# Tile ends moved two rows later and spread over five rows, and 32 weight blocks read from a compact copy, in a two-block transformer kernel on one core

## The reference

```python
for l in range(DEPTH_2):                        # one layer
    x = x + hybrid_mixer(rmsnorm_2(x, norm_mix_w[l]), w_in[l], ...)       # gated delta rule | LRU, then @ w_out
    x = x + memory_cross_attention(rmsnorm_2(x, norm_xattn_w[l]), ...)    # wq, wkv, wo
    x = x + peer_ffn(rmsnorm_2(x, norm_ffn_w[l]), peer_wq[l], peer_subkeys[l], peer_u[l], peer_v[l])
return rmsnorm_2(x, norm_final_w)

def peer_ffn(h, wq, subkeys, u_tab, v_tab):     # 16384 experts of one neuron each
    q = (t @ wq).reshape(ntok, PEER_HEADS, 2, PEER_DH)
    ...                                         # two top-16 lists per head -> 8*16 = 128 expert numbers per token
    act = jax.nn.gelu(jnp.einsum('phkd,pd->phk', u_tab[ib], tb)) * gb
    return jnp.einsum('phk,phkd->pd', act, v_tab[ib])
```

## Time and profile before

| | us |
|---|---|
| median of 3 runs (4435.22 to 4448.99) | 4435.89 |
| profiled execution | 4437.59 |
| its span | 4435.8 |
| PE busy | 3636.4 (82%) |
| DVE busy | 2022.3 (46%) |
| POOL busy | 1391.2 (31%) |
| ACT busy | 1006.3 (23%) |
| first u gather to the end of the span | 2739.9 to 4435.8 |

### The profile page before, as it was taken

How to read it: one execution, slowest core, us unless ns; L and a number is a source line. 1 busy time by engine, 2 the same in 40 slices (tenths; PEclk the granted TensorE clock), 3 DMA queues, 4 the chain that set the end, 5 groups by cost and what they waited for, 6 DMA issues and landing times.

```text
span 4435.8 us, 45304 instructions
## 1 busy us (share of the span) xinstructions
PE 3636.4 (82%) x16837; PEld 2072.6 (47%) x16837; DVE 2022.3 (46%) x4634; ACT 1006.3 (23%) x2265; POOL 1391.2 (31%) x1494
## 2 busy tenths in 40 slices
PE   7788998999999778999997989767777766555655
PEld 4455534555555565444456877434544433111111
DVE  3565062623222583111125324577756555665553
ACT  3664032200000211100015122344123112112111
POOL 0000001162422000000000002656656776777776
PEclk9899999999999899999998989888889888666677
DMA  4331102222122133422212134989779998999998
GB/s 178 114 114 44 57 24 50 76 109 105 68 83 111 62 118 124 140 79 80 80 64 76 58 133 152 339 317 327 273 295 389 359 400 322 360 357 335 357 368 313
DMA packets 287765, 821.56 MB, mean 185 GB/s; under 512 B 24040, under 2 KB 60340, under 8 KB 284244
## 3 DMA queue, kind: packets, MB, share of 16 engines
q0 software_dynamic: 150832, 565.17, 34.4%
q1 hardware_dynamic: 136320, 253.22, 16.0%
q10 hardware_dynamic: 420, 0.62, 0.1%
HBM read 791.67 MB, written 27.26 MB: 185 GB/s over the span
## 4 chain that ended last, share of the span: by engine, by line
PE 57%; DVE 13%; POOL 9%; issue 8%; ACT 5%; DMA 4%; another core or an unknown queue 3%; SPq 0%; DVEq 0%; ACTq 0%; POOLq 0%
PE bank L728 25%; PE bank L2627 6%; POOL arena L1176 5%; POOL ring L1167 4%; PE bank L2863 4%; PE bank L2430 3%; PE bank L2587 3%; DVE ring L2286 2%; PE bank L2482 2%; DMA arena<-in_peer_v,arena 1%; PE bank L2345 1%; PE bank L593 1%; PE bank L2422 1%; PE bank L2722 1%
## 5 line engine op out<-in xcount | busy, mean ns | idle before, releaser
L2863 PE MATMUL bank<-arena 64*64 64x512 f32 x4096 | 684.4, 766 | 383.4 <-issue 318.5
L1167 POOL DMA_INDIRECT ring<-in_peer_u,arena x512 | 560.2, 1094 | 1389.3 <-DVE arena L2233 1061.8
L2286 DVE SCALAR_TENSOR_TENSOR ring<-ring,xT 128x1024 f32<-128x1024 f32 x512 | 615.4, 1223 | 271.7 <-DMA ring<-in_peer_u,arena 247.3
L1176 POOL DMA_INDIRECT arena<-in_peer_v,arena x512 | 581.4, 1135 | 207.3 <-issue 145.9
L2863 PEld LDWEIGHTS bank<-arena 64*64 64x64 f32 x4096 | 183.1, 160 | 800.6 <-issue 798.0
L728 PE MATMUL bank<-hT,ring 128*128 128x512 f32 (+1 forms) x1536 | 553.0, 522 | 5.1 <-ACT hT L643 5.1
L728 PE MATMUL bank<-arena,ring 128*128 128x512 f32 (+1 forms) x1536 | 551.3, 521 | 0.0
L728 PEld LDWEIGHTS bank<-hT,ring 128*128 128x128 f32 x1536 | 292.5, 191 | 263.9 <-issue 250.7
L728 PEld LDWEIGHTS bank<-arena,ring 128*128 128x128 f32 x1536 | 291.8, 190 | 258.1 <-issue 244.0
L2627 PE MATMUL bank<-hT,ring 128*128 128x256 f32 x1536 | 366.6, 397 | 51.5 <-DMA ring<-in_peer_wq 14.6
L2627 PEld LDWEIGHTS bank<-hT,ring 128*128 128x128 f32 x1536 | 300.4, 199 | 140.4 <-issue 59.5
(11 more groups left out here) (520 smaller groups left out, 4591.6 us busy)
## 6 DMA issues: line engine op xcount, KB each, us to landing
ring<-in_mlp_w SPq DMA_DIRECT2D x32, 2048.0 KB, 8.3
ring<-in_ada_w SPq DMA_DIRECT2D x24, 2048.0 KB, 13.3
s_store<-arena POOLq DMA_DIRECT2D x8, 2816.0 KB, 9.6
ring<-in_w_in SPq DMA_DIRECT2D x10, 2048.0 KB, 7.9
arena<-s_store SPq DMA_DIRECT2D x16, 1024.0 KB, 6.9
ring<-in_w_in SPq DMA_DIRECT2D x12, 1024.0 KB
ring<-in_w_out SPq DMA_DIRECT2D x4, 2048.0 KB, 8.1
ring<-in_s_w_glu SPq DMA_DIRECT2D x4, 2048.0 KB, 14.3
```

Source lines behind the costliest of these rows:

```text
L1167: pool.indirect_dma_start(u_row[k % ERING], None, I["peer_u_2"][0], bass.IndirectOffsetOnAxis(idxs[:, k // EXPERTS, k % EXPERTS:k % EXPERT ...
L1176: pool.indirect_dma_start(v_row[v % ERING], None, I["peer_v_2"][0], bass.IndirectOffsetOnAxis(idxs[:, v // EXPERTS, v % EXPERTS:v % EXPERT ...
L2286: dve.scalar_tensor_tensor(row, row, 1.0, h_tok[k // EXPERTS % 2], ALU.mult, ALU.mult, accum_out=dots[k // AGROUP % 2][:, k % AGROUP:k % A ...
L2863: last = pe.matmul(banks[2 * r + n][QUADS[r if y == 0 else 1 - r], :], diag[QUADS[r], s, :], v_row[s][QUADS[r], 512 * n:512 * n + 512], st ...
```

## The change

It has two parts that don't touch each other.

**Tile ends.** `tile_end` gives each engine the rows: for tile 0 everything stands in one row, k = 137; for tiles 1 to 3 the swap stands at 128(T+1)+10, `final_rows` and the root two rows later, the scale four rows later. ScalarE's squares now stand right behind its swap. The loop is five ticks longer; no row is processed in them. TensorE's and GpSimd's instructions don't change.

**Weights.** Early in SyncE's stream, behind the loads of `w_in_r` and ahead of those of block one's `w_out`, 32 transfers copy the 32 blocks within device memory into `weights_kept`, where a partition's 2048 values lie in one piece of 8 KB. The 32 loads of the gather stage read from there.

```diff
+TILE_END = {"swap": 0, "rows": 2, "scale": 4}
+def tile_end(k, step):
+    for t in range(NL // P):
+        if k == (t + 1) * EXPERTS + TILE_LAG + (TILE_END[step] if t else -1):
+            return t
+    return None
...
-        TICKS = range(ROWS + TILE_LAG)
+        TICKS = range(ROWS + TILE_LAG + 5)
...
+            for b, (name, a) in enumerate(TAIL_WEIGHTS):
+                sp.dma_start(weights_kept[b].rearrange("p (k n) -> p k n", k=KD),
+                             I[name][0].rearrange("(k p) n -> p k n", p=P)[:, :, a:a + 256]).then_inc(S("weights_kept"), 16)
             for j in range(2):
                 load_block(sp, block0["w_out"] + j, I["w_out"][0].rearrange("(k p) n -> p k n", p=P)[:, :, j * 512:(j + 1) * 512])
...
+            def kept_blocks(name, lo, hi):
+                for j in range(lo, hi):
+                    load_block(sp, block0[name] + j, weights_kept[tail_at[name] + j])
...
-            mix_blocks(1, 0, 3)
+            sp.wait_ge(S("weights_kept"), 16 * len(TAIL_WEIGHTS))
+            kept_blocks("mix1", 0, 3)
...
-            tail_blocks(1, "pq1", "peer_wq_2", 256)
+            kept_blocks("pq1", 0, 8)
...
-                if k % EXPERTS == TILE_LAG - 2 and k > EXPERTS:
-                    final_swap(k // EXPERTS - 1)
-                if k % EXPERTS == TILE_LAG - 1 and k > EXPERTS:
-                    final_rows(k // EXPERTS - 1)
+                if tile_end(k, "swap") is not None:
+                    final_swap(tile_end(k, "swap"))
+                if tile_end(k, "rows") is not None:
+                    final_rows(tile_end(k, "rows"))
+                if tile_end(k, "scale") is not None:
+                    final_scale(tile_end(k, "scale"))
```

More of the change, by code:

```diff
@@ L906, in build @@
         kv_made, kv_kept = at(14336, 4096), nc.dram_tensor("kv_kept", (P, 4096), F32).ap()
+        TAIL_WEIGHTS = [*[("w_in_2", (2056, 2568, 0, 512, 1024, 1536)[j // 2] + 256 * (j % 2)) for j in range(12)],
+                        *[(name, 256 * j) for name, n in (("w_out_2", 4), ("xattn_wq_2", 4), ("xattn_wo_2", 4), ("peer_wq_2", 8)) for j in range(n)]]
+        tail_at = {"mix1": 0, "w2_1": 12, "xq1": 16, "wo1": 20, "pq1": 24}
+        weights_kept = nc.dram_tensor("weights_kept", (len(TAIL_WEIGHTS), P, KD * 256), F32).ap()
         xkT = [x[:, 0:2048].rearrange("p (k n) -> p k n", k=KD) for x in (kv_made, ring[:, 3])]
@@ L1018, in mask_loads, with tail_blocks @@
                     sp.dma_start(mask(h, j), cst(name)).then_inc(S("g_masks"), 16)
-            def tail_blocks(h, name, src, width, lo=0, hi=None):
+            def tail_blocks(name, src, lo=0, hi=None):
                 w = I[src][0].rearrange("(k p) n -> p k n", p=P)
[L1022 to L1026, removed]
+                for j in range(lo, hi or w.shape[2] // 512):
+                    load_block(sp, block0[name] + j, w[:, :, j * 512:(j + 1) * 512])
+            mix_blocks(0, 2)
+            mix_blocks(2, 3)
             for n in range(8):
@@ L1029, in _ @@
             mask_loads(0)
-            mix_blocks(0, 3, 6)
-            tail_blocks(0, "xkv", "xattn_wkv_2", 512)
-            tail_blocks(0, "w2_0", "w_out_2", 512)
+            mix_blocks(3, 6)
+            tail_blocks("xkv", "xattn_wkv_2")
+            tail_blocks("w2_0", "w_out_2")
             for n in range(8):
@@ L1049, in _ @@
                         sp.dma_start(gate_rows(1, a, m)[64 * b:64 * b + 64, 64 * b:64 * b + 64], I[name][0, 2 * m + b]).then_inc(S("lru_landed"), 16)
-            mix_blocks(1, 3, 6)
+            kept_blocks("mix1", 3, 6)
             filled(sp, ticket0["lg1_3"] + 1)
             mask_loads(1)
-            mix_blocks(1, 6, 12)
+            kept_blocks("mix1", 6, 12)
             filled(sp, ticket0["so1_3"])
-            tail_blocks(1, "w2_1", "w_out_2", 256)
-            tail_blocks(1, "xq1", "xattn_wq_2", 256)
+            kept_blocks("w2_1", 0, 4)
+            kept_blocks("xq1", 0, 4)
             for m in range(KD):
@@ L1591, in _ @@
             for k in TICKS:
-                if k % EXPERTS == TILE_LAG - 2 and k > EXPERTS:
-                    final_swap(k // EXPERTS - 1)
-                if k % EXPERTS == TILE_LAG - 1 and k > EXPERTS:
-                    final_root(k // EXPERTS - 1)
+                if tile_end(k, "swap") is not None:
+                    final_swap(tile_end(k, "swap"))
+                    final_squares(tile_end(k, "swap"))
+                if tile_end(k, "rows") is not None:
+                    final_root(tile_end(k, "rows"))
+                if tile_end(k, "scale") is not None:
+                    final_scale(tile_end(k, "scale"))
                 d = k - DIAG_LAG
@@ L2264, in final_rows, with final_scale @@
                     emptied(dve, ticket0[f"ffn{T_}"] + x)
+            def final_scale(T_):
                 dve.wait_ge(S("fin_act"), 7 * T_ + 6)
```

19 lines of the change are left out of this document (10 added, 9 removed).

## The result

The changed kernel takes 4421.79 us (median of 15 runs, 4399.85 to 4433.70), the kernel before, run beside it, 4442.29 (15 runs, 4433.72 to 4466.35). The ratio is 0.9939, with a 95% interval of 0.9924 to 0.9953: 27 us faster by that ratio, which weighs all runs, where 26.5 were forecast; the two medians lie 20.5 us apart, and the changed kernel's own median is 11 us above the 4411 of the forecast and within its range. Runs of one kernel on one chip lie up to 37 us apart, so the parts of those 27 us can be told only by ratios of many runs, and by stretches of the traces that are short against them. The profiled execution took 4421.62 us with a span of 4419.8.

A forecast was written before the change was run, and what follows sets the result against it. The gather stage was taken as bound by moving rows (DMA), with GpSimd's issuing close behind. Terms -9.2 - 6.6 - 11.7 + 1.0 = -26.5 on 4437.59 gave 4411 us; likeliest case 4400 to 4422, 8 in 10 4388 to 4434.

The forecast's parts named there:

- Tile ends: Gather stage, ends of tiles 0 to 2: filling VectorE's swap waits gives -4.3 - 5.9 + 1.0 = -9.2 us; bounds 0 and -21.
- Rival B: Ends of tiles 1 and 2: the stall moves from u to v and costs as much, 4420 us; chance 0.10.
- Copies: From 366.3 us, before w_out is needed: copies are covered, their traffic costs +1 us; bounds 0 and +10.
- Rival D: Early part: copies hold up w_out and TensorE waits 85 us, 4495 us; chance 0.05.
- Fewer DMA microseconds: Gather stage's weight loads: 8 KB pieces save 0.33 us a block, -6.6 us over 20 blocks; bounds 0 and 10.5.
- Earlier landing: Gather stage's weight loads: blocks land sooner, shortening TensorE's waits, -11.7 us together; bounds 0 and -34.6.
- The first wait: TensorE's 13.97 us wait for the load issued at 2802.63: landing in 9 us instead of 15.8, 6.8 us earlier.
- the second wait: TensorE's wait at 3314.64: goes wholly, 6.06 us, but counted as 4.9 because the DMA engines are full around it.
- The third wait: TensorE's 14.60 us wait at 3547.52: gains 0, since the DMA engines are full on both sides.
- Rival A: Weight loads: the landing doesn't move the end, so -11.7 goes, 4423 to 4426 us; chance 0.20.
- C: Gather stage: more gain than counted, from all waits and packets; 4384 us, more likely 4395; chance 0.09.
- E: Gather stage: bursts of 8 KB pieces delay u rows by up to 2.8 us a block, 4467 us; chance 0.06.

The follow-up runs named there:

- Experiment 1: The kernel before with only the tile ends of the change, weights loaded as before and nothing copied: ratio 0.9987 to the kernel before.
- experiment 9: The changed kernel run again as it is, in the last group of runs: ratio 0.9934 to the kernel before, 4323.05 us.
- experiment 12: The changed kernel with the ends of tiles 1 and 2 spread but begun two rows earlier (offsets -2, 0, 2): ratio 0.9955 to the kernel before.
- 8: The changed kernel with kept weight blocks read in pieces of 2 KB: ratio 0.9946 to the kernel before.
- 6: The changed kernel with the 32 copies issued by GpSimd in the second MLP: ratio 0.9940 to the kernel before.
- 11: The changed kernel with tile ends moved but not spread and copies issued by GpSimd in the second MLP: ratio 0.9919 to the kernel before, 4318.73 us.
- 0: The kernel before, without the change: 4442.29 us, median of 15 runs beside the changed kernel.
- 3: The kernel before with the 32 copies added and nothing reading them: ratio 1.0011 to the kernel before.
- 4: The changed kernel with compact kept blocks loaded in 1 KB pieces standing 64 bytes apart: ratio 1.0006 to the kernel before.
- 7: The changed kernel with all 32 copies made but only the twelve w_in_2 blocks loaded from them: ratio 0.9975 to the kernel before.
- A: The changed kernel, with both parts of the change: 4421.79 us, ratio 0.9939 to the kernel before.
- 2: The kernel before with only the 32 copies and the loads in 8 KB pieces, tile ends as before: ratio 0.9952 to the kernel before.
- 5: The changed kernel with tile ends moved by two rows but not spread (offsets 0, 0, 0): ratio 0.9927 to the kernel before.

## Why the prediction was right

**Tile ends.** Forecast -9.2. Experiment 1 gives -6 (-14 to +2), experiments 9 against 12 give -8 to -10, the stretches -4.8 - 3.5 = -8.3. In the pair of traces before and after, the mechanism shows step by step: most of the wait is filled, `final_rows` of tile 2 was put at 4071.9 on the scale of before, which is 4058.8 after the 13.1 us by which row 392's u issue came earlier, and TensorE started at 4059.56; v row 392 gained 4.2 us (4.3 forecast) and v row 264 gained 5.9 (5.9). That it fits to 0.1 us is luck of this pair, since experiment 1 has 0.9 and 5.5. u row 408 was 14.8 us ahead where row 392 had been 13.1, so some of it was given back behind the end. The waits at the two swaps fell under 5 us as the sign asked, to 3.24 and none, but 6.14 us stand just ahead of the swap of tile 1 and 4.46 us in the key choice of tile 2. Tile 0's forecast loss of 1 us can't be told: rows 120 to 152 take 128.6 us before and 128.3 after, and between 125.7 and 138.0 in experiments 1 to 8. Rival B, the stall in v costing as much, falls with experiment 12: it is there, 7.93 and 3.61 us where 4 to 9 were reckoned, and costs less. The lower bound of -21 took GpSimd's wait at tile 2 (8.2 us) for VectorE's, which was 14.82; nothing else rests on it.

**Copies.** Forecast +1, from 366 to at most 580; they ended at 476, at 3.4 us a block near the lower end of the bounds. Rival D is out by a wide margin: even 64 copies were done by 578. One sign of being wrong did appear, the gather stage starting later than 2743 us (2743.85). It was badly chosen: that start lies anywhere from 2738.2 to 2743.5 in the kernels without early copies (before, 1, 6, 11), and from 2737.7 to 2744.1 in those with them.

**Fewer DMA microseconds.** This is the mis-sized term. Forecast 0.33 us a block, from the row of loads in 6 and 8 KB pieces. Measured on the weights' own queue: (14.7 - 12.2)% of 220 us = 5.5 us for ten blocks, 0.55 each, 11 us for 20 blocks and not 6.6. The stand-in still had 6 KB pieces and other rows; whether that is the whole difference was not tried. The term also left out that the gathers beside the small pieces take longer. In rows 152 to 192 it was 8 x 0.33 = 2.6 us by the forecast and 8.9 by the traces.

**Earlier landing.** Forecast -11.7. The first wait held in size: 9 us from issue to use forecast, 8.6 measured, and 7.1 to 8.7 in all nine traces that load it in 8 KB pieces. The 13.97 us wait became 6.74, and the stretch over it fell by 5.7 us (6.8 forecast), some of it fewer DMA microseconds. For the second wait I counted no more than the hole of 4.9 us, and left out a wait of 6.11 us for `xattn_wq_2` that no row of mine showed; TensorE's timeline before has it:

```profile
3388.69 5.29 PE L2627 MATMUL bank<-hT,ring 128*128 128x256 f32 x16 [6.11 <-DMA ring<-in_xattn_wq]
```

Both waits went, 12.2 us of TensorE's, and the stretch over them fell by 13.6 us instead of 7.5. It is tempting to set the two equal, but the DMA engines are the limit there: holes gave 4.7 us, so the cap was right, and the rest of the miss belongs to the term above. The third wait was put at 0: after had u row 232 20.1 us ahead of before and row 264 13.1 again. Over all traces rows 216 to 264 take 147.3 us on average with the old form (0, 1, 3, 4, 7) and 145.6 with the new (A, 2, 5, 6), which themselves reach from 139.5 to 149.4.

**The sum.** The forecast was tile ends -9.2, weights -18.3, copies +1. The runs say -6 to -10 and, with the copies, -21 (-14 to -29). That the total fell on the forecast to 1 us by the ratio, and to 6 by the medians, is luck within these; each term has its sign, and the packets' term was too small where the landing's was somewhat too large. Rival A's number is refuted by experiment 2. But its thought, that full engines hand the time back, holds for the waits behind row 152, where TensorE's 12.2 us bought 4.7. No run separates the two ways in which larger pieces help, since experiments 4 and 8 change both; the split is an estimate from shares of the traces. C falls too, since its 4395 would be a ratio of 0.9904, outside the interval, and E, bursts that delay rows, isn't seen: rows 24 to 40, 152 to 192 and 216 to 264 are all shorter on average with 8 KB pieces.

## What to carry over

When DMA engines are shared by queues, look at the size of the pieces of each and not only at bytes: here 1 KB pieces beside gathers of 4 KB ones landed 1 MB in 16 to 17 us, 2 KB in 12.3, and 8 KB in 7 to 9, and most of the gain was there at 2 KB. Where the engines are full, count the gain in DMA microseconds (share times length), those of the other queues too, and not in the waits that go away. A weight block that is read late can be copied to such a form while the engines idle early. Where an engine waits at a seam, move work that doesn't need the seam ahead of it, above all what stands between the seam's first and last step; spreading the seam's own steps showed no gain.

## What was not expected of the hardware

- Small pieces also hold up the sync engine. The eight small `lru_wa` loads behind two weight blocks take 16.01 us to issue before, 16.72 with compact 1 KB pieces, 8.26 with 2 KB and 5.23 with 8 KB.
- GpSimd's gather issue, 0.94 us alone, takes longer beside VectorE's dot products, and in three places it ended 0.82 to 0.83 us behind the end of one: at 4053.40 + 3.48 = 4056.88, where the second dot product ends at 4054.85 + 1.21 = 4056.06; at 3667.46 + 3.07 = 3670.53, with a dot product ending at 3669.71; at 3620.00 + 3.49 = 3623.49 in experiment 9, with one ending at 3622.66. Two rows put right behind the swap so cost GpSimd 2.1 to 2.6 us, which may be why the spread brings nothing. It wasn't tested by itself.
- The same kernel took 2% less in the last group of runs, and nearly all of it is the gather stage: 1639.2 us from the first u issue to the last in the first trace after, 1547.6 in experiment 9. Experiments 5 to 8 and 9 to 12 have the same chip number, so whether another chip or another state of one made the difference isn't shown. In a stretch of rows alone, windows of experiment 9 show 389 GB/s at a DMA share of 1.01, where 354 at 0.96 stood above:

```profile
3700.00:3900.00 200.00, 108.30 (x617) 31.71 (x615) 135.62 (x371) 31.80 (x104) 154.91 (x149) 0.78 1.01 389
```
